# Pairing the transposes of two attention heads around the value products of the pair ahead

## The reference, cut to what matters

```python
# local (na): 8 heads, window of 16 columns, bias from a table
sc = jnp.einsum('bhjqd,bhrjkd->bhjqrk', qblk, k_blk, preferred_element_type=jnp.float32)
sc = jnp.where(mask, sc + bias[None].astype(jnp.float32), -jnp.inf)
p = jax.nn.softmax(sc.reshape(sc.shape[:4] + (wr * NA_KCOLS,)), axis=-1).reshape(sc.shape)
return jnp.einsum('bhjqrk,bhrjkd->bhjqd', p.astype(v_blk.dtype), v_blk)
...
# causal (mla): 8 heads of 96 (64 + 32 rotated), values of 64
s = jnp.einsum('bqhd,bkhd->bhqk', q_blk, k).astype(jnp.float32)
s = jnp.where(key_idx[None, :] <= q_idx[:, None], s, NEG_INF)
p = jax.nn.softmax(s, axis=-1).astype(v.dtype)
return jnp.einsum('bhqk,bkhd->bqhd', p, v)
```

## Time and profile before

| | before |
|---|---|
| median of 3 runs | 1658.93 us |
| profiled execution | 1660.57 us |
| its span | 1658.7 us |
| PE busy | 1629.4 us, 98% |
| weight loads busy | 1591.4 us, 96% |
| DVE busy | 1157.1 us, 70% |
| ACT busy | 868.7 us, 52% |
| mean granted TensorE clock | 0.996 |
| local set, layer 0 | about 158 to 235 us of the span |
| local set, layer 1 | about 711 to 790 us |
| causal set | about 1229 to 1297 us |

### The profile page before, as it was taken

How to read it: one execution, slowest core, us unless ns; L and a number is a source line. 1 busy time by engine, 2 the same in 40 slices (tenths; PEclk the granted TensorE clock), 3 DMA queues, 4 the chain that set the end, 5 groups by cost and what they waited for, 6 DMA issues and landing times.

```text
span 1658.7 us, 32250 instructions
## 1 busy us (share of the span) xinstructions
PE 1629.4 (98%) x13674; PEld 1591.4 (96%) x13674; DVE 1157.1 (70%) x1734; ACT 868.7 (52%) x1302; POOL 40.0 (2%) x59
## 2 busy tenths in 40 slices
PE   9999999999999999999999999999999999999998
PEld 8999999999999999999999999998989999999998
DVE  6678778657566767877874966677576545877777
ACT  5456544645444454555355654445745555465554
POOL 3000000003000000000000000000000000000000
PEclk9999999999999999999999999999999999999999
DMA  9854457536656465545664465555545454546562
GB/s 314 288 178 153 153 196 249 187 126 193 227 175 207 161 236 163 162 144 190 203 239 144 160 222 181 201 181 164 178 146 167 152 178 140 179 153 204 178 205 100
DMA packets 82798, 305.84 MB, mean 184 GB/s; under 512 B 10688, under 2 KB 10816, under 8 KB 80480
## 3 DMA queue, kind: packets, MB, share of 16 engines
q1 hardware_dynamic: 77008, 279.44, 50.7%
q0 software_dynamic: 5648, 24.35, 4.9%
HBM read 300.52 MB, written 6.29 MB: 185 GB/s over the span
## 4 chain that ended last, share of the span: by engine, by line
PE 88%; DVE 9%; issue 2%; ACT 1%; DVEq 0%; ACTq 0%
PE general L617 55%; PE general L621 14%; PE scores L659 5%; DVE weights_lo L1584 3%; PE attention_out L659 3%; PE probs_transposed L659 3%; PE attention_out L811 2%; PE scores L744 1%; PE probs_transposed L763 1%; PE scores L835 1%; ACT weights_hi L1154 1%; PE general L690 1%; PE probs_transposed L617 1%; DVE x_tok L1655 1%; DVE x_tok L1652 1%
## 5 line engine op out<-in xcount | busy, mean ns | idle before, releaser
L1584 DVE TENSOR_TENSOR weights_lo<-raw_weights,weights_hi 128x1024 fp32r<-128x1024 f32 x525 | 633.5, 1222 | 387.0 <-ACT weights_hi L1154 384.9
L1154 ACT ACTIVATE weights_hi<-raw_weights 128x1024 fp32r<-128x1024 f32 x525 | 553.3, 1057 | 402.3 <-PE general L617 227.2
L617 PE MATMUL general<-xT_hi_part,weights_hi 128*128 128x256 f32 x2432 | 682.8, 281 | 5.2 <-DVE weights_lo L1584 2.7
L617 PE MATMUL general<-xT_lo_part,weights_hi 128*128 128x256 f32 x2432 | 675.7, 278 | 0.0
L617 PE MATMUL general<-xT_hi_part,weights_lo 128*128 128x256 f32 x2432 | 675.6, 278 | 0.0
L617 PEld LDWEIGHTS general<-xT_hi_part,weights_hi 128*128 128x128 f32 x2432 | 458.8, 189 | 13.6 <-issue 8.5
L617 PEld LDWEIGHTS general<-xT_lo_part,weights_hi 128*128 128x128 f32 x2432 | 458.4, 188 | 0.4
L617 PEld LDWEIGHTS general<-xT_hi_part,weights_lo 128*128 128x128 f32 x2432 | 458.4, 189 | 0.0
L1927 DVE SCALAR_TENSOR_TENSOR exp_ring<-general,param_cols,exp_ring 128x255 f32<-128x255 f32 (+1 forms) x176 | 76.7, 477 | 43.4 <-ACT exp_ring L1343 41.9
L1343 ACT ACTIVATE exp_ring<-general,param_cols 128x256 f32<-128x256 f32 x88 | 44.9, 561 | 66.5 <-PE general L617 66.4
L621 PE MATMUL general<-weights_hi,xT_hi_part 128*128 128x256 f32 x272 | 76.9, 283 | 1.0 <-DVE xT_lo_part L1615 1.0
(11 more groups left out here) (318 smaller groups left out, 2935.3 us busy)
## 6 DMA issues: line engine op xcount, KB each, us to landing
raw_weights<-in_stream SPq DMA_DIRECT2D x525, 512.0 KB, 4.3
attention_area<-in_ln_rows POOLq DMA_DIRECT2D x9, 1024.0 KB, 5.4
bias_scratch<-in_rpb POOLq DMA_DIRECT2D x32, 96.0 KB, 11.8
attention_area<-bias_scratch POOLq DMA_DIRECT2D x2, 1536.0 KB, 8.2
memT_hi<-memT_scratch POOLq DMA_DIRECT2D x2, 1024.0 KB, 5.3
memT_lo<-memT_scratch POOLq DMA_DIRECT2D x2, 1024.0 KB, 9.0
attention_area<-in_mem SPq DMA_DIRECT2D x1, 1024.0 KB, 5.2
z_tok<-in_x SPq DMA_DIRECT2D x1, 1024.0 KB, 8.9
```

The costliest lines, as they stand in the source:

```text
L617: ins = nc.tensor.matmul(ps[b][0:m, half * T:half * T + T], w[wk][:, half * m:half * m + m], x[xk_], start=first, stop=last, skip_group_ch ...
L1154: nc.scalar.activation(hi_half(h), raw_half(h), ACT.Copy).then_inc(*hi_done.more())
L1584: nc.vector.tensor_tensor(lo_half(h), raw_half(h), hi_half(h).bitcast(F32), ALU.subtract).then_inc(*lo_done.more())
```

## The change

In the local and causal sets, PE's two `turn`s of a pair move into one odd step: `turn` of the even head, the values of the pair ahead, `turn` of the odd head. The first pair has no values ahead of it, so its two `turn`s follow each other (in the local set `ya_squares` follows behind both). Even steps have no `turn`. The causal set's scores are now written a pair at a time in even steps, though still by the single-head function. ACT's `probs_out` and DVE's `normed` follow the same order, with ACT's `attn_out` between the two copies. Nothing is computed more or less.

```diff
@@ attention on PE @@
                 js = set_jobs(name)
                 for step in range(len(js) + 2):
-                    if step < len(js) and name not in ("da", "na"):
+                    if step < len(js) and name == "mla":
+                        for m in range(2 if step % 2 == 0 else 0):
+                            scores(js[step + m])
+                    elif step < len(js) and name not in ("da", "na"):
                         scores(js[step])
                     elif step < len(js) and step % 2 == 0:
                         scores_of_pair(js[step])
...
                     if step >= 2 and name not in ("na", "mla"):
                         values(js[step - 2])
-                    elif step >= 3 and step % 2 == 1:
-                        values_of_pair(js[step - 3])
-                    if 1 <= step <= len(js):
+                    if name in ("na", "mla"):
+                        if step % 2 == 1 and step < len(js):
+                            turn(js[step - 1])
+                            if step >= 3:
+                                values_of_pair(js[step - 3])
+                            turn(js[step])
+                    elif 1 <= step <= len(js):
                         turn(js[step - 1])
                     if step in extra:
                         extra[step]()
@@ attention on ACT @@
                         for i in (4, 5):
                             filler(("dk", i))
+                    if name in ("na", "mla"):
+                        if step % 2 == 1 and step < len(js):
+                            probs_out(js[step - 1])
+                        if step >= 2:
+                            attn_out(js[step - 2])
+                        if step % 2 == 1 and step < len(js):
+                            probs_out(js[step])
+                        if step in extra:
+                            extra[step]()
+                        continue
                     if step >= 2 and name != "dil":
                         attn_out(js[step - 2])
@@ attention on DVE @@
                     if step < len(js):
                         maxima(js[step])
-                    if 1 <= step <= len(js):
+                    if name in ("na", "mla"):
+                        if step % 2 == 1 and step < len(js):
+                            normed(js[step - 1])
+                            normed(js[step])
+                    elif 1 <= step <= len(js):
                         normed(js[step - 1])
```

## The result

| | before | after |
|---|---|---|
| median | 1659.01 us (4 runs, 1657.93 to 1662.61) | 1679.87 us (4 runs, 1678.27 to 1682.15) |
| profiled execution | 1660.57 us | 1679.63 us |
| its span | 1658.7 us | 1677.8 us |
| mean granted TensorE clock | 0.996 | 0.996 |

The ratio is 1.0127, 95% interval 1.0114 to 1.014: the changed kernel is 20.9 us slower. The forecast was 15.7 us slower, 1674.6 us. The direction was right and the size 5.2 us short: the time lies 0.13 us inside the upper end of the whole range (1668 to 1680), but outside the range of the forecast's own mechanism (1671 to 1678, the waits with none or one fall of the clock).

What follows compares the result with a forecast made beforehand. PE, busy 98% of the span, was taken as the bound. Local sets 9.1, causal set 5.1 and one clock fall 1.5 made 15.7 us on 1660.57: 1676.3, or 1674.6 us on the median's scale; range 1668 to 1680.

Steps and rivals of the forecast that it cites:

- One bank for two transposes: In every lot, PE's second transposes wait until ACT has copied the first; 12 places, PE starting 0.06 us behind the copy.
- Local set: Four lots of each local set, waits less removed lone lots: +1.9, +0.7, +0.5, +1.4 us, 9.1 for two sets.
- The fourth lot: Last lot of a local set: a second split ahead of the gate's evacuation adds 0.7 us, bounds 0 and 0.95; +1.4 altogether.
- Causal set's waits: Causal set, waits less removed lone lots: +2.3 us in the first lot, +0.9 in each other, sum 5.1.
- The clock: Idle PE in the first lots halves the granted clock; one fall taken, +1.5 us, bounds 0 and 4.5.
- The pace: Rival: projections in or behind the sets flip between 0.118 and 0.113 us a matmul; 5 us, 1680 or 1670; chance 0.13.
- Weights late: Rival: half a split, 0.48 us, stands open at nine lots behind the first ones; +4 us, 1679; chance 0.09.
- More clock falls: Rival: the clock falls at all three first lots, perhaps after a middle wait; 3.0 us more, 1677.6; chance 0.06.
- Not slower: Rival: ACT copies the first head before PE finishes the values, all waits go; 1657.5 or 1656 us; chance 0.06.

Runs made afterwards that it cites:

- two_banks: Changed kernel, but the odd head of a lot is transposed into a free projection bank, so it waits for no copy; 1666.07 us, ratio 1.004.
- causal_only: Kernel before with the change in the causal set only, local sets in the old order; 1664.82 us, ratio 1.0036.
- busy_first: Changed kernel with seven more identity matmuls between the two groups of transposes of each first lot; 1677.51 us, ratio 1.0106.
- early_copy: Changed kernel, but ACT's weight split moves behind the first copy of a lot; 1672.06 us, ratio 1.0072.
- last_lone: Changed kernel, but the last pair of each set keeps its two separate transposes; 1675.47 us, ratio 1.0102.

## Where the prediction was right, and the step that failed

**One bank for two transposes: right.** All 12 waits came. PE goes on 0.14 us behind the end of the copy (229.27 against 228.55 + 0.58), where 0.06 had been read from the earlier trace rows: a miss of 0.08 us a place, which the sums of the local sets don't show. At the three first lots they sum to 1.83 + 1.83 + 2.46 = 6.1 us (forecast about 5.7), at the rest to 4 x 0.76 + 2 x 1.38 + 3 x 1.03 = 8.9 (7 to 9). two_banks took them away and with them most of the loss.

**Local set: right.** +4.55 and +4.15 us for 4.55, where the missing 0.4 in layer 1 is the pace inside the set. The fourth lot, for which only bounds of 0 and 0.95 were to be had, took 0.62 us more than the middle ones, against 0.7. The reason given holds: ACT waits 2.46 us for DVE ahead of the last exponentials, and both splits then stand in front of the gate.

**Causal set's waits: right, 0.7 us low.** 8.3 less 3.1 for the clock is 5.2, for 5.1, but that closeness is luck: the set won 0.6 us by the pace, and without it the waits and lots cost 5.8. causal_only and busy_first give 5.9 each in the same way. Of the 0.7 us, 0.3 are the first lot, where the second transposes began 2.95 us behind the first and 2.67 had been read.

**The clock: mechanism right, price too low.** One fall was forecast and one came, in the causal set's first lot and nowhere else in the changed places. Its cost was read from a stretch of 3 us at half clock, 1.5 us. Two of the three profiled executions of the changed kernel had it so, the one shown here had it twice as long, 3.1. The bounds counted falls of one size; a long fall was not among them. Yet the trace of before had one, which the prediction overlooked, ahead of the causal set:

```profile
1204.00:1208.00 4.00, 3.65 (x9) 1.16 (x8) 2.96 (x4) 1.57 (x3) 0.00 (x0) 1.00 0.64 205
1208.10:1214.80 6.70, 5.50 (x22) 4.73 (x23) 6.25 (x11) 0.00 (x0) 0.00 (x0) 0.50 0.20 70
```

It is there in all 18 profiled executions, before and after, and so costs nothing in the comparison. The Trainium skill (TensorE: Matmul & The Clock Gate, section "HAM oscillation — how this bites in real kernels"), whose rule warns only of longer gaps, was rightly overruled by the row with 2.11 us: the clock fell behind 2.46 us in all six profiled executions that have this wait.

**The pace: the step that failed.** The projections behind the local sets were costed at nothing. Every matmul outside the lots entered the sum at the pace that it had before; the runs showed 504 matmuls behind each local set at 0.1178 us for 0.1133, 4.7 us together, in all three profiled executions of the changed kernel. A rival had named the two paces and given a change 0.13. Its 5 us and 1680 came out almost to the digit, but partly by luck: it counted the 576 matmuls inside a set, and there the changed kernel ran no slower in the pair of executions shown. It said that the paces change at lots, while they also change without one (last section). It also took the pace for a coin with two sides. Behind the local sets it is none: three executions of the changed kernel agree, and so do two of the one before. Inside the sets it does change between executions of one kernel: layer 0's set took 81.31, 82.15 and 81.26 us, and the middle one had 0.8 us of slow pace.

How much of the miss is the pace can be estimated from the traces. Take all matmuls of 128x256, with start-to-start distances of 0.105 to 0.125 us, and sum what each has over 0.1133. That gives 23.3 and 22.5 us in the two executions of before, and 26.3, 28.3 and 26.2 in the three of the changed kernel: about 4.0 us more, less than the 4.7 behind the sets, since other stretches ran faster. The forecast was 5.2 us short; by this estimate 4.0 of it are the pace, 0.7 the clock (on average 2.2 for 1.5) and 0.7 the causal set's waits. These three make 5.4.

What could have been seen beforehand: the kernel before ran the 504 matmuls behind each local set at the faster of its two paces, so a change of pace there could only cost time.

**The other rivals.** Weights late: the waits for them are unchanged, 5.4 us. More clock falls: none at the local first lots (1.77 to 1.84 us in the three profiled executions). Not slower: it needed a copy 1.9 us earlier at the first lots; early_copy gave 0.95 of it.

## What to carry to other kernels

- Two users of a single buffer placed close together turn a free wait into a paid one. Its price is read from the engine that frees the buffer: what stands in its program order ahead of the release, here one 0.95 us split. Pairing the work itself gave nothing that could be measured once the wait was gone.
- Before moving work in a stream with no slack, look at the start-to-start distance of its plain instructions on either side. If the stretch behind is at the faster of the paces seen, there is only something to lose.
- Prices read from one execution for things of chance (a fall of the clock) need both a short and a long case in the range.

## What the runs showed of the hardware that was not expected

- Two paces of the same matmul (128x256) at the granted clock of 1.00: 0.1133 and 0.1178 us start to start. Behind the local sets a stretch keeps one for all 504 matmuls. Elsewhere the pace also changes without a lot or a wait, where PE goes from projections of one line to those of another. In the kernel before, the matmuls of L621 from 295.00 to 299.83 us stand 0.1178 us apart and those of L617 from 300.41 to 302.00 stand 0.1136 apart:

```profile
295.00 0.28 PE L621 MATMUL probs_transposed<-weights_hi,memT_hi 128*128 128x256 f32 x1
299.83 0.28 PE L621 MATMUL probs_transposed<-weights_hi,memT_lo 128*128 128x256 f32 x1
300.41 0.28 PE L617 MATMUL general<-xT_lo_part,weights_hi 128*128 128x256 f32 x1
302.00 0.28 PE L617 MATMUL general<-xT_hi_part,weights_hi 128*128 128x256 f32 x1
```

Some stretches differ between executions of one kernel (behind the changed kernel's second lot in layer 0: 0.1133 twice, 0.1178 once), others never did. For an isolated matmul of 256 columns the Trainium skill (TensorE: Matmul & The Clock Gate, section "Back-to-back issue gap") gives 256 / 2.4 + 2.5 = 109.2 ns; for streams of weight loads and matmuls it has about 81 ns at 128 columns and 131 ns at 512. No stretch of 128x256 matmuls here ran at 109.2 ns; both paces are longer and lie between the two figures for streams.

- Idle time of PE and the fall of the clock: in the causal set's first lot, 2.45 or 2.46 us brought it in six profiled executions out of six, 2.26 us didn't in the one that had it. Nor is idle time needed: ahead of the causal set the clock fell for 6.8 us in all 18 profiled executions. In last_lone that fall began at 1215.0 us, with no idle time over 0.2 us in the 10 us before it; PE had matmuls on 32 rows from 1212.12 us on, and projections on 128 rows ahead of them. In the feed-forward of layer 0 length did not decide: behind 1.83 us it fell (causal_only), and behind 2.50 us it did not. The changed kernel's row, and the three us behind it:

```profile
417.68 0.36 PE L659 MATMUL scores<-weights_hi,ffn_act_hi 128*128 128x256 f32 x1 [2.50 <-issue]
```

```profile
418.00:421.00 3.00, 3.00 (x29) 3.00 (x28) 2.87 (x3) 1.06 (x1) 0.00 (x0) 1.00 1.00 240
```
